# First projection chunk of a hybrid encoder kernel: token tiles normed one by one, first weights in two halves, narrow weights made on GpSimd, more dummy transposes

## The reference

```
def rms_norm(x, g):
    y = xf * lax.rsqrt(jnp.mean(xf * xf, axis=-1, keepdims=True) + EPS)
    return (y * g.astype(jnp.float32)).astype(x.dtype)

def mixer_sublayer(x, norm_g, w_in, conv_w, gate_bias, head_norm_g, w_out):
    hn = rms_norm(x, norm_g)
    proj = jnp.einsum('bsd,de->bse', hn, w_in)
    gb, gc, u, q, k, v, o, gates = jnp.split(proj, SPLITS, axis=-1)
    ... a gated short convolution of gb, gc and u; an mLSTM scan of q, k, v in two directions ...
    return x + jnp.einsum('bse,ed->bsd', mix, w_out)

def expert_choice_sublayer(x, norm_g, w_router, w_gate, w_up, w_down):
    ... softmax router, each of 16 experts takes its top tokens, SwiGLU experts, weighted sum ...
```

## Time and profile before

| what | value |
|---|---|
| median of 3 runs | 1298.23 us (1298.19 to 1299.98) |
| the profiled execution's own time | 1298.81 us |
| its span in the profile | 1297.1 us |
| PE busy | 1255.2 us, 97% of the span |
| DVE, ACT, POOL busy | 905.8, 742.0, 323.1 us |
| mean granted TensorE clock | 0.985 |
| chain that ended last | PE 92%, DMA 2%, ACT 2%, DVE 2%, issue 1% |

### The profile page before, as it was taken

One profiled execution on the slowest core, in us unless ns is written; L12 is line 12 of the kernel. 1 busy time (PEld: TensorE's weight loads), 2 busy tenths in 40 slices (PEclk: granted clock), 3 DMA queues, 4 the chain that ended last, 5 costly groups with the idle time before them and its releaser, 6 DMA issues.

```text
span 1297.1 us, 25116 instructions
## 1 busy us (share of the span) xinstructions
PE 1255.2 (97%) x9762; PEld 1032.7 (80%) x9814; DVE 905.8 (70%) x1298; ACT 742.0 (57%) x1079; POOL 323.1 (25%) x316
## 2 busy tenths in 40 slices
PE   8999999999999999779999999999999999999994
PEld 7868986666687888578888888898889888988892
DVE  6462122541586655978879888988898889888887
ACT  7645322222345544456677667766676667667764
POOL 2512221010133231141132313131313231223040
PEclk8999999999999999979999999999999999999998
DMA  8231544360278773288999999999999999999996
GB/s 274 66 122 50 163 146 137 108 180 25 75 248 248 226 213 116 90 302 290 329 300 315 327 332 294 321 333 319 299 315 340 313 306 318 332 310 309 295 351 271
DMA packets 242033, 314.76 MB, mean 243 GB/s; under 512 B 16097, under 2 KB 206049, under 8 KB 241969
## 3 DMA queue, kind: packets, MB, share of 16 engines
q1 hardware_dynamic: 226576, 268.54, 62.3%
q0 software_dynamic: 15392, 45.36, 12.0%
HBM read 274.41 MB, written 39.44 MB: 242 GB/s over the span
## 4 chain that ended last, share of the span: by engine, by line
PE 92%; DMA 2%; ACT 2%; DVE 2%; issue 1%; SPq 0%; POOL 0%; ACTq 0%; DVEq 0%; POOLq 0%
PE psum L2253 23%; PE psum L2114 15%; PE psum L2260 11%; PE psum L2081 9%; PE psum L1965 9%; PE psum L2276 9%; PE psum L2294 4%; PE psum L2285 4%; PE psum L2246 1%; PE psum L2027 1%; DMA eraw<-in_w_up_dram 1%; PE psum L2032 1%; ACT yt L1248 1%; PE psum L1987 1%; PE psum L1945 1%
## 5 line engine op out<-in xcount | busy, mean ns | idle before, releaser
L1812 DVE TENSOR_TENSOR elo<-eraw,ehi 128x2048 bf16<-128x2048 f32 x192 | 433.5, 2285 | 1.0 <-POOLq L822 1.0
L1218 ACT ACTIVATE ehi<-eraw 128x2048 fp32r<-128x2048 f32 x192 | 362.2, 1902 | 25.7 <-PE psum L2294 18.6
L2253 PE MATMUL psum<-xc,ehi 128*128 128x320 f32 x2048 | 332.3, 314 | 1.9 <-DVE xc L1817 1.9
L2253 PEld LDWEIGHTS psum<-xc,ehi 128*128 128x128 f32 x2048 | 304.2, 189 | 3.5 <-DVE xc L1817 2.3
L2260 PE MATMUL psum<-xb,elo 128*128 128x160 bf16 x2048 | 163.9, 233 | 0.0
L1825 DVE TENSOR_REDUCE gu<-psum 128x320 f32<-128x640 f32 x128 | 105.3, 823 | 82.0 <-PE psum L2260 81.8
L2260 PEld LDWEIGHTS psum<-xb,elo 128*128 128x128 bf16 x2048 | 138.5, 98 | 13.0
L2114 PE MATMUL psum<-hn_nar,wnar 128*128 128x512 bf16 (+1 forms) x748 | 141.2, 343 | 1.2
L2276 PE MATMUL psum<-ehi,hc 128*128 128x512 f32 x512 | 132.7, 406 | 0.0
L2114 PEld LDWEIGHTS psum<-hn_nar,wnar 128*128 128x128 bf16 x768 | 73.1, 98 | 63.0 <-issue 4.5
L2276 PEld LDWEIGHTS psum<-ehi,hc 128*128 128x128 f32 x512 | 95.2, 188 | 22.1
(11 more groups left out here) (290 smaller groups left out, 1664.2 us busy)
## 6 DMA issues: line engine op xcount, KB each, us to landing
eraw<-in_w_gate_dram SPq DMA_DIRECT2D x64, 1024.0 KB, 6.6
eraw<-in_w_up_dram SPq DMA_DIRECT2D x64, 1024.0 KB, 9.6
eraw<-in_w_down_dram SPq DMA_DIRECT2D x64, 1024.0 KB, 13.6
wraw<-in_w_in_dram SPq DMA_DIRECT2D x12, 1024.0 KB, 7.3
negm<-negm_d SPq DMA_DIRECT2D x10, 512.0 KB, 7.4
acc_d<-x POOLq DMA_DIRECT2D x10, 512.0 KB, 5.4
tok_d<-tk POOLq DMA_DIRECT2D x10, 512.0 KB, 2.9
v<-v_d SPq DMA_DIRECT2D x18, 256.0 KB, 4.3
```

The lines of the kernel that those rows point to most:

```text
L1218: act.activation(f["ehi"][:, j % RING, :], f["eraw"][:, raw_slot(s, j), :], ACT.Copy).then_inc(S["ehi"], 1)
L1812: dve.tensor_tensor(f["elo"][:, j % RING, :], f["eraw"][:, raw_slot(s, j), :], f["ehi"][:, j % RING, :].bitcast(F32), ALU.subtract).then_i ...
L2253: pe.matmul(o[:, 0:2 * NC], hi[:, k, c], x[:, k, :, :].rearrange("p a t -> p (a t)"), start=(k == 0), stop=False, skip_group_check=True)
```

## The change

- `BATCHES` now begins with four batches of one tile (tiles 0, 1, 2, 3), then pairs. Each of the first four tiles has its own load semaphore, its own root on ACT and its own five small operations on DVE.
- SP issues tile 0, tile 1, the gains and gate columns, then chunk 0's weights as two DMAs of 0.5 MB (k 0 to 3 on `w_first`, k 4 to 7 on the old semaphore), then the other tiles with no wait between.
- HIGH of `wnar` for chunks 0 and 1 is made by POOL (`weights_narrow`, four casts of 128x1024, two a chunk) and no more by ACT. Those of chunk 0 stand between POOL's casts of tiles 0, 1 and 2; those of chunk 1 ahead of the store of group 7.
- ACT copies out tiles 0 and 1 ahead of its half of `whi`, and takes the sums of tiles 2 to 5 behind it.
- DVE scales tile 0 ahead of the gate columns' product, and needs only the first half of the weights for its half of `whi`. The rest of its order is the old one.
- PE: 44 dummy transposes, tile 0, 4 dummies, tile 1, 6 dummies. The high products of groups 0 and 1 are cut in two by k (`high_first_tiles`), so that k 0 to 3 of both tiles need only `w_hid`.

The core of the diff (left out: names of semaphores, the same edits in ACT's list of `split_narrow(1)`, and the tail of DVE's list):

```diff
-    BATCHES = [(n, n + 2) for n in range(0, NT, 2)]
+    BATCHES = [(n, n + 1) for n in range(4)] + [(n, n + 2) for n in range(4, NT, 2)]
...
             load_tokens(0)
+            load_tokens(1)
...
-            load_chunk(0)
-            sp.wait_ge(w_ind[0], 16)
-            for i in range(1, len(BATCHES)):
+            for k0, landed in ((0, S["w_first"]), (4, w_ind[0])):
+                sp.dma_start(b["wraw"][:, 0, k0:k0 + 4, :], w_in[0, k0 * P:(k0 + 4) * P, chunks[0][1]:chunks[0][1] + CH]
+                             .rearrange("(k p) n -> p k n", p=P)).then_inc(landed, 16)
+            for i in range(2, len(BATCHES)):
                 load_tokens(i)
...
+            def weights_narrow(j, k0, k1):
+
+                pool.wait_ge(S["w_hid"] if (j, k0) == (0, 0) else S["w_hi"], j + 1)
+                pool.tensor_copy(wnar[j][:, HIGH, k0:k1, 0:CH], whi[j][:, k0:k1, 0:CH].bitcast(F32)
+                                 ).then_inc(S["w_nar01"], 1)
...
-            for n in range(3):
-                tokens_narrow(n)
+            tokens_narrow(0)
+            weights_narrow(0, 0, 4)
+            tokens_narrow(1)
+            weights_narrow(0, 4, KD)
+            tokens_narrow(2)
...
+                if i == of_chunk[0][7]:
+                    weights_narrow(1, 0, 4)
+                    weights_narrow(1, 4, KD)
...
-            token_sums(0, 0, 2)
-            root(0)
+            for i in range(2):
+                token_sums(i, *BATCHES[i])
+                root(i)
...
-            split_high(0, 4, KD)
             tokens_high(0)
             tokens_high(1)
-            split_narrow(0)
-            token_sums(1, 2, 4)
-            root(1)
-            token_sums(2, 4, 6)
-            root(2)
+            split_high(0, 4, KD)
+            for i in range(2, 5):
+                token_sums(i, *BATCHES[i])
+                root(i)
+            tokens_high(2)
             evict(0)
             evict(1)
-            tokens_high(2)
             tokens_high(3)
...
+            token_roots(0)
+            scale_rows(*BATCHES[0])
             dve.wait_ge(S["g1_in"], 32)
...
-            token_roots(0)
-            scale_rows(0, 2)
-            dve.wait_ge(w_ind[0], 16)
+            token_roots(1)
+            scale_rows(*BATCHES[1])
+            dve.wait_ge(S["w_first"], 16)
...
-            token_roots(1)
-            scale_rows(2, 4)
-            token_roots(2)
-            scale_rows(4, 6)
+            for i in range(2, 5):
+                token_roots(i)
+                scale_rows(*BATCHES[i])
             tokens_low(2)
             tokens_low(3)
...
+            def high_first_tiles():
+
+                for k0 in (0, 4):
+                    pe.wait_ge(S["w_hi"] if k0 else S["w_hid"], 1)
+                    for g in range(2):
+                        pe.wait_ge(S["hn_hi"], g + 1)
+                        for k in range(k0, k0 + 4):
+                            pe.matmul(result(g), b["hn_hi"][:, k, g * P:(g + 1) * P], whi[0][:, k, 0:CHG], start=(k == 0),
+                                      stop=False)
+
             def low_first_tiles():
 
-                pe.wait_ge(S["w_nar"], 1)
+                pe.wait_ge(S["w_nar01"], 2)
...
-            for _ in range(48):
-                pe.transpose(psum[:, 7, 0:P], ident[:, :], ident[:, :])
+            dummies(44)
             transpose_tokens(0)
+            dummies(4)
             transpose_tokens(1)
+            dummies(6)
```

More of the change, by code:

```diff
@@ L329, in hybrid_conv_mlstm_moe @@
             "bar act_ch dve_ch pool_ch "
-            "x_in0 x_in1 x_in2 x_in3 x_in4 g1_in g1_small const zeroed small_in sumsq rooted xn_done xT_ps hn_hi hn_lo hn_nar "
-            "w_in0 w_in1 gT_ps w_hid w_hi w_lo w_nar proj ev_act ev_dve st0 st1 st2 st3 "
+            "x_in0 x_in1 x_in2 x_in3 x_in4 x_in5 x_in6 g1_in g1_small const zeroed small_in sumsq rooted xn_done xT_ps hn_hi hn_lo hn_nar "
+            "w_in0 w_in1 w_first w_nar01 gT_ps w_hid w_hi w_lo w_nar proj ev_act ev_dve st0 st1 st2 st3 "
             "soft rows_t rows_exp rows_nat rows_out colT_ps "
@@ L346, in hybrid_conv_mlstm_moe @@
             "conv_done cvl_done aff_out g2b_in tk_scaled gf_in f_in0 f_in1 f_in2 f_in3 f_in4 f_sum f_root f_y f_out f_out_p f_gath f_same f_row f_sq f_quart f_done f_set").split()}
-        x_in = (S["x_in0"], S["x_in1"], S["x_in2"], S["x_in3"], S["x_in4"])
+        x_in = (S["x_in0"], S["x_in1"], S["x_in2"], S["x_in3"], S["x_in4"], S["x_in5"], S["x_in6"])
         w_ind, stg = (S["w_in0"], S["w_in1"]), (S["st0"], S["st1"], S["st2"], S["st3"])
@@ L904, in split_narrow @@
                 act.wait_ge(S["w_hi"], j + 1)
-                if j == 0:
-                    act.wait_ge(S["w_hid"], 1)
                 act.activation(wnar[j % 2][:, HIGH, :, 0:CH], whi[j % 2][:, :, 0:CH].bitcast(F32), ACT.Copy
@@ L959, in _ @@
             act.wait_ge(S["g1_in"], 32)
-            split_high(0, 4, KD)
             tokens_high(0)
             tokens_high(1)
-            split_narrow(0)
-            token_sums(1, 2, 4)
-            root(1)
-            token_sums(2, 4, 6)
-            root(2)
+            split_high(0, 4, KD)
[3 more added lines that the diff above has]
+            tokens_high(2)
             evict(0)
             evict(1)
-            tokens_high(2)
             tokens_high(3)
-            token_sums(3, 6, 8)
-            root(3)
+            token_sums(5, *BATCHES[5])
+            root(5)
             evict(2)
             tokens_high(4)
-            token_sums(4, 8, NT)
-            root(4)
+            token_sums(6, *BATCHES[6])
+            root(6)
             evict(3)
@@ L987, in _ @@
             tokens_high(8)
-            split_narrow(1)
             evict(7)
@@ L1391, in _ @@
             tokens_low(1)
-            token_roots(1)
-            scale_rows(2, 4)
-            token_roots(2)
-            scale_rows(4, 6)
+            for i in range(2, 5):
+                token_roots(i)
+                scale_rows(*BATCHES[i])
             tokens_low(2)
             tokens_low(3)
-            token_roots(3)
-            scale_rows(6, 8)
+            token_roots(5)
+            scale_rows(*BATCHES[5])
             tokens_low(4)
-            token_roots(4)
-            scale_rows(8, NT)
+            token_roots(6)
+            scale_rows(*BATCHES[6])
             for n in range(5, 8):
@@ L2070, in high_part @@
                 t0, w = tokens_in(i)
-                if i == 0:
-                    pe.wait_ge(S["w_hid"], 1)
                 if j == 0:
@@ L2107, in low_part @@
                     pe.wait_ge(S["w_lo"], j + 1)
-                    pe.wait_ge(S["w_nar"], j + 1)
+                    if j < 2:
+                        pe.wait_ge(S["w_nar01"], 2 * j + 2)
+                    else:
+                        pe.wait_ge(S["w_nar"], j - 1)
                 for k in range(KD):
@@ L2119, in _, with dummies @@
             AFTER.update({n - 2: (n,) for n in range(4, NT)})
-            for _ in range(48):
-                pe.transpose(psum[:, 7, 0:P], ident[:, :], ident[:, :])
+            def dummies(n):
+                for _ in range(n):
+                    pe.transpose(psum[:, 7, 0:P], ident[:, :], ident[:, :])
+            dummies(44)
             transpose_tokens(0)
+            dummies(4)
             transpose_tokens(1)
+            dummies(6)
             for i, (j, kind, part, m, t0, w) in enumerate(pgroups):
@@ L2138, in _ @@
                     pe.wait_ge(S["ev_act"] if who == "act" else S["ev_dve"], c)
[L2139 to L2142, removed]
+                if i == 0:
+                    high_first_tiles()
+                elif i == 1:
+                    low_first_tiles()
                 elif i % 2:
```

## The result

The changed kernel takes 1301.84 us (median of 9 runs, 1299.14 to 1304.93), the kernel before 1298.22 (9 runs, 1297.49 to 1299.98). The ratio is 1.0026, with a 95% interval of 1.0017 to 1.0036: slower by 3.6 us. Predicted were 1302.4, +4.2. The profiled execution took 1301.09, span 1299.4, which is 2.3 above that of before.

A forecast was written before the change was run, and what follows sets the result against it. PE's start of group 2's LOW products, delayed by DVE's chain, was taken as the bound: -1.4 + 3.25 + 0.5 + 1.9 = +4.25, so 1298.2 + 4.2 = 1302.4 us; range 1296.4 to 1305.4, the forecast's own 1300.8 to 1304.5.

The forecast's parts named there:

- The bound: Ahead of group 2's LOW products, DVE's chain gets longer, so PE starts them at about 29.6 instead of 25.35.
- The early start: On DVE, `whi` starts at 9.8 instead of 11.20, from single tiles and weights in halves: -1.4 us.
- GpSimd's casts of weights and first tiles: Casts hold up DVE's `whi` (1.0) and `split_low` (3.0); the gate subtraction meets none (0.75 back): +3.25 us, bounds -0.75 to +3.25.
- One round more: On DVE before `tokens_low(2)`, three rounds of small operations and four scalings take 5.7 us instead of 5.23: +0.5.
- The casts of tiles 2 and 3: They fall on DVE's third round and the scaling of tiles 4 and 5: +0.9 and +1.0, bounds 0 and 1.9.
- clock on top: Rival, chance 0.13: PE's idle stretches bring half rate behind 29.6, costing up to 3.4; sum +6 to +7.5, about 1305.
- The sum: At PE's start of group 2's LOW products: -1.4 + 3.25 + 0.5 + 1.9 = +4.25 us, carried to the end.
- Nothing held up: Rival, chance 0.17: casts don't delay DVE's `split_low`, `whi` or small operations; DVE -1.65, time 1296.6 or 1295.5.
- Held up once only: Rival, chance 0.15: a run of casts costs DVE's four operations one wait, not three; +1.25 for +3.25, sum +2.2 (1300.4).

The follow-up runs named there:

- the second profile: The changed kernel, unaltered, run once more for a further profile: 1302.39 us.
- the memsets: The changed kernel with GpSimd's two weight casts of chunk 0 replaced by memsets of zero, those narrow HIGH weights left out: 1298.25 us, one execution.
- ACT's part undone: The changed kernel, but ACT again makes the narrow HIGH weights of chunk 0, behind its half of `whi`: 1301.08 us, ratio 1.0024.
- the upper four: Slower runs of the changed kernel with tiles 2 and 3 in one batch (median 1299.20 us): four at 1301.33 to 1301.55, the other seven 1297.80 to 1299.43.
- the kernel with the casts moved: The changed kernel with chunk 0's narrow HIGH weights on ACT, tiles 2 and 3 one batch, waits ahead of casts of tiles 0, 1, 2, 4, 5: 1297.49 us.

## Why the prediction was right, and where its sum was not

**The bound.** Right in kind. DVE's chain became the longer one ahead of group 2's LOW products: 25.35 became 26.40 and, in the second profile, 26.33 followed by half rate. But this is +1.0 of the forecast's +4.25: `tokens_low(2)` was forecast for 28.3 and started at 25.12 and 25.06, hardly behind the 25 below which the prediction called itself wrong.

**The early start.** Predicted -1.4, measured -1.65 (11.20 to 9.55).

**GpSimd's casts of weights and first tiles.** The mechanism was right, the size too large: predicted +3.25, measured +0.8 (`whi` 1.92 for 1.14), +2.4 (`split_low` 4.01 to the next start for 1.59) and -0.7 (gate), together +2.5. A meeting cost 0.8 us and not the 1.0 of the sum, four times. In the second profile there were three meetings and not four, +1.6 in all. `tokens_low(1)` was over at 19.56 instead of the predicted 20.75. The Trainium skill, SBUF — State Buffer, section "SBUF: two separate sides", names two SBUF inputs against a GpSimd operation that reads SBUF; the memsets agree (0.47 us beside one, 1.26 beside a cast).

**One round more.** Predicted +0.5, measured +0.3: 5.56 us from 19.56 to 25.12, against 5.23.

**The casts of tiles 2 and 3.** This term was wrong in the first profile: predicted +1.9, measured 0. The prediction let PE transpose tile 2 at full rate. It ran at half rate from 18 to 21, began tile 2's transposes only at 22.76, and its cast came at 24.93, when the scaling was nearly over. Where PE was on time the meeting took place: 0.8 us in the second profile, 0.9 and 1.06 with ACT's part undone. So "clock on top" is not simply a cost to be added: in the first profile it is lost time on PE and at the same time keeps tile 2's cast off the scaling.

**The sum.** From these terms the first profile has -1.65 + 2.5 + 0.3 = +1.15, and PE's start moved by 1.05; the predicted +4.25 is in neither of the two profiles. Chunk 0 ends 1.4 and 2.7 late in them. In the first that is the 1.05 and a stop ahead of group 5 that grew from 0.46 to 0.79, where the prediction only let it move along; in the second it is 1.0 and the 1.67 of half rate. The executions themselves were 2.3 and 3.6 above the profiled one of before. The rest, 0.9 in both, lies further on, and its cause stays open. In the first there is a wait of 0.9 for a DMA at 391 us (`sts`), which shows in some of the profiles, of faster kernels too, and in the second there is none; but where the expert products begin (578 us before) the two are 1.8 and 2.9 late, and where they end (1264) 2.3 and 3.6. That the median's +3.6 comes so near to the forecast's +4.2 is luck: terms that were too large stand for half rate and later stretches that the sum had at nothing.

**The rivals.** Nothing held up: refuted. Held up once only: refuted, three times in line. The clock: seen at 26 to 29 in the second profile, where it cost 1.67 and not up to 3.4. With tiles 2 and 3 in one batch it is seen in the one profiled execution of the upper four; their mean granted clock was 0.984 to 0.986, that of the lower seven 0.986 to 0.988, and some 3 us lie between the two groups.

## What to carry to other kernels

Before work is moved to GpSimd to relieve another engine, list what VectorE does at that moment: here operations with two SBUF inputs and the scalings from SBUF to SBUF waited for a cast to end, about 0.8 us a meeting, and `tokens_low`, which reads PSUM and one SBUF operand, did not. A wait that puts such a cast beside the harmless ones can make a kernel faster. If a chain is shortened, ask what now arrives earlier beside it: the same cast that was harmless at 24.9 cost 0.9 us at 21.9.

## What the runs showed that I had not expected

Filling PE's idle time helped where I saw nothing to fill it for. With PE idle for 1.0 us at most at a time (the kernel with the casts moved), 14 dummies took 0.7 us off the median and 2.5 off the slowest execution, though the profile of that kernel shows full rate without them; by what, no run shows. And one round of small operations less was worth 2.6 us in the medians, where its five operations are 1.0; the four executions of the upper group, 3 us slower, show that this figure hangs on the clock too.
